# First attention block of a two-block decoder kernel: half of the modulation by dot products, and a new order of VectorE's, ScalarE's and TensorE's work in it

## What is computed

```python
mod = silu(c) @ ada_w[0] + ada_b[0]                  # 1024 -> 6 * 1024
sh1, sc1, g1, sh2, sc2, g2 = split(mod, 6)
h = rmsnorm(x, norm_g) * (1 + sc1) + sh1
proj = h @ w_in                                       # 1024 -> 384 + 256 + 32
c_q, c_kv = rmsnorm(proj[:, :384]), rmsnorm(proj[:, 384:640])
k_rope = apply_rope(proj[:, 640:])
q  = (c_q  @ w_uq ).reshape(256, 16, 64 + 32)         # rope on the last 32
kv = (c_kv @ w_ukv).reshape(256, 16, 64 + 64)         # k_nope, v
o = softmax(mask(q k^T * scale)) v                    # 16 heads, two blocks of 128 queries
x = x + g1 * (o @ w_out)
```

## Time and profile before

| | us |
|---|---|
| Median of three timed runs | 2814.59 |
| The profiled execution | 2818.61 |
| Its span | 2816.8 |
| PE busy / DVE busy / ACT busy | 2649.1 / 1961.2 / 1562.6 |

### The profile page before, as it was taken

The page is one execution under the profiler, slowest core; times in us unless marked ns, Lnnn a source line. Parts: engine busy times, 40 slices in busy tenths (PEclk is TensorE's granted clock), DMA queues, the critical chain, the costliest instruction groups (busy, mean ns, idle before and its releaser), DMA issues.

```text
span 2816.8 us, 39113 instructions
## 1 busy us (share of the span) xinstructions
PE 2649.1 (94%) x15496; PEld 2307.9 (82%) x15496; DVE 1961.2 (70%) x2819; ACT 1562.6 (55%) x2264; POOL 10.9 (0%) x24
## 2 busy tenths in 40 slices
PE   7788998888999999999996999999999999999998
PEld 3677998876788888888885998887898998887898
DVE  3768877766698898899897556655555556656555
ACT  2443445554687777777775445465444445465444
POOL 0000000000000000000000000000000000000000
PEclk9789998999899999999998999999999999999999
DMA  8537984514699999999996665534565665434563
GB/s 277 189 114 267 346 307 128 150 60 142 240 365 335 332 369 339 337 354 352 335 357 214 196 186 174 155 93 134 166 186 156 196 186 174 150 98 128 162 186 116
DMA packets 349600, 616.35 MB, mean 219 GB/s; under 512 B 20706, under 2 KB 174882, under 8 KB 349410
## 3 DMA queue, kind: packets, MB, share of 16 engines
q1 hardware_dynamic: 346402, 603.35, 64.4%
q0 software_dynamic: 1872, 5.99, 0.7%
q10 hardware_dynamic: 1136, 4.44, 0.4%
HBM read 612.66 MB, written 1.05 MB: 218 GB/s over the span
## 4 chain that ended last, share of the span: by engine, by line
PE 87%; DVE 7%; ACT 3%; issue 1%; DMA 1%; DVEq 0%; ACTq 0%
PE pb L286 25%; PE pb L287 25%; PE pb L288 25%; PE pb L292 9%; PE pb L408 2%; DVE parts L260 2%; ACT parts L245 1%; PE pb L2204 1%; PE pb L2660 1%; DMA X<-in_x 0%; DVE hTl L421 0%; DVE raw L625 0%; ACT pb L478 0%; DVE xn L509 0%; DVE xn L512 0%
## 5 line engine op out<-in xcount | busy, mean ns | idle before, releaser
L260 DVE TENSOR_TENSOR parts<-raw,parts 128x1024 fp32r<-128x1024 f32 (+2 forms) x1051 | 1264.7, 1216 | 593.1 <-ACT parts L245 559.2
L245 ACT ACTIVATE parts<-raw 128x1024 fp32r<-128x1024 f32 (+2 forms) x1051 | 1102.7, 1054 | 829.0 <-PE pb L288 706.4
L286 PE MATMUL pb<-parts,arenar 128*128 128x512 f32 (+2 forms) x1696 | 669.1, 395 | 14.7 <-DVE arenar L421 6.1
L287 PE MATMUL pb<-parts,arenar 128*128 128x512 f32 (+2 forms) x1696 | 650.7, 384 | 0.0
L288 PE MATMUL pb<-parts,arenar 128*128 128x512 f32 (+2 forms) x1696 | 649.8, 383 | 0.0
L286 PE MATMUL pb<-hTh,parts 128*128 128x256 f32 x1952 | 559.8, 287 | 7.4 <-DVE hTl L421 5.1
L287 PE MATMUL pb<-hTl,parts 128*128 128x256 f32 x1952 | 558.4, 286 | 0.0
L288 PE MATMUL pb<-hTh,parts 128*128 128x256 f32 x1952 | 558.3, 286 | 0.0
L286 PEld LDWEIGHTS pb<-hTh,parts 128*128 128x128 f32 x1952 | 381.4, 195 | 11.7 <-issue 7.2
L286 PEld LDWEIGHTS pb<-parts,arenar 128*128 128x128 f32 x1696 | 322.0, 190 | 80.7 <-issue 16.7
L287 PEld LDWEIGHTS pb<-hTl,parts 128*128 128x128 f32 x1952 | 381.3, 195 | 1.8
(11 more groups left out here) (286 smaller groups left out, 1972.4 us busy)
## 6 DMA issues: line engine op xcount, KB each, us to landing
raw<-in_moe_w_gate SPq DMA_DIRECT2D x176, 512.0 KB, 5.2
raw<-in_moe_w_up SPq DMA_DIRECT2D x176, 512.0 KB, 5.2
raw<-in_moe_w_down SPq DMA_DIRECT2D x176, 512.0 KB, 5.2
raw<-in_ffn_wg SPq DMA_DIRECT2D x88, 512.0 KB, 4.1
raw<-in_ffn_wu SPq DMA_DIRECT2D x88, 512.0 KB, 3.7
raw<-in_ffn_wd SPq DMA_DIRECT2D x88, 512.0 KB, 4.4
raw<-in_ada_wT SPq DMA_DIRECT2D x80, 512.0 KB, 5.2
raw<-in_w_in SPq DMA_DIRECT2D x72, 512.0 KB, 3.7
```

What stands on the lines that cost most here:

```text
L245: a.e.activation(self.part(t, 0), self.slot(t), ACT.Copy).then_inc(*a.up(self.c.hi, t.m))
L260: v.e.tensor_tensor(self.part(t, 1), self.slot(t), self.part(t, 0).bitcast(F32), ALU.subtract).then_inc(*v.up(self.c.lo, t.m))
L286: e.matmul(o, a[0], b[0], start=start, stop=False, skip_group_check=True)
L287: e.matmul(o, a[0], b[1], start=False, stop=False, skip_group_check=True)
```

## The change

It has five parts. (1) The shift's eight plain tiles are replaced by eight dot tiles of the same size. Four of them stand among the scale's eight tiles, four behind. VectorE makes their dots, TensorE only spreads the resulting columns over rows. (2) Dots get a walk of their own (`dots`); `low` can be told not to do those ahead of it, as long as an assertion holds that they are fewer than six tiles behind. (3) Before the loop, all latents are turned and cut as they come, the common key's rope is made before q's, its turned copy before the first kv product; the lows of m = 1 and 2 stand between the pieces of xn. (4) In the loop each slot begins with the head's maximum, then come sums, one low, dots, values; on ScalarE the exponentials stand ahead of the cut. `q_dve` and `kT_dve` follow slot h+2. (5) The 24 dot tiles have other places in the stream: one ahead of m = 4 to 10 and 12 to 14, two ahead of 15 to 21.

```diff
-    def low(self, v, times=1):
-        while times and self.n_low < len(self.tiles):
-            t = self.tiles[self.n_low]
-            self.n_low += 1
-            if t.kind == "dot":
-                v.wait_ge(*self.landed(t))
-                self.dot(v, t, self.slot(t))
...
+    def low(self, v, times=1, dots=True):
+        for t in self.cut[self.n_lo:self.n_lo + times]:
+            while dots and self.n_dot < len(self.dotted) and self.dotted[self.n_dot].n < t.n:
+                self.dots(v)
+            assert all(x.n > t.n - self.nraw for x in self.dotted[self.n_dot:]), t.label
...
+    def dots(self, v, times=1):
+        for t in self.dotted[self.n_dot:self.n_dot + times]:
+            self.n_dot += 1
+            v.wait_ge(*self.landed(t))
+            self.dot(v, t, self.slot(t))
...
-    FIRST = (2, 3, 0, 1)
+    FIRST = (2, 3)
...
+        shift = self.K.dot_tiles(0)
+        mixed = sum(([*scale[2 * i:2 * i + 2], shift[i]] for i in range(4)), [])
+        return mixed + self.K.dot_tiles(1)
...
+        for n in range(2):
+            b = K.c.bk[4 + n]
+            t.wait_ge(*K.c.dv.val(("col", n)))
+            t.wait_ge(*b.turn(("ada", n)))
+            for j in range(4):
+                m = mm1(t.e, b.t[:, j * P:(j + 1) * P], K.acols[:, 4 * n + j:4 * n + j + 1].to_broadcast([P, P]),
+                        K.C["ident"])
+            m.then_inc(*t.up(K.c.pe, ("ada", n)))
...
-        dots = {4: 1, 5: 1, 6: 1, 7: 1, 22: 1, 23: 1} | {m: 2 for m in range(13, 22)}
+        dots = {m: 1 for m in (4, 5, 6, 7, 8, 9, 10, 12, 13, 14)} | {m: 2 for m in range(15, 22)}
...
-    def slot_dve(self, v, h):
+    def slot_dve(self, v, h, lows=0, dots=0):
         if h < 16:
             self.att.max_dve(v, h)
         if 1 <= h <= 16:
             self.att.sums_dve(v, h - 1)
+        self.K.W.low(v, lows, False)
+        self.K.W.dots(v, dots)
...
# TensorE
         self.c_pe(t, 0)
+        self.c_pe(t, 4)
         self.q_pe(t, 0)
-        self.c_pe(t, 4)
-        self.kv_pe(t, 0)
         t.wait_ge(*c.dv.val("kr"))
         K.turn_pe(t, "krT", 6, [self.kr[:, tt, :] for tt in range(2)])
+        self.kv_pe(t, 0)
...
# ScalarE
         self.in_act(a, 0)
-        K.W.hi(a, 2)
         self.c_act(a, 0)
         self.in_act(a, 1)
+        self.c_act(a, 4)
         K.root_act(a, "c", slice(0, 4))
         K.W.hi(a, 2)
-        self.c_act(a, 4)
+        K.W.hi(a, 2)
...
+            self.slot_act(a, h)
             K.W.hi(a)
             self.kv_act(a, g)
-            self.slot_act(a, h)
-            K.W.hi(a)
             self.slot_act(a, h + 1)
             K.W.hi(a)
             self.slot_act(a, h + 2)
+            K.W.hi(a)
             self.slot_act(a, h + 3)
...
# VectorE
-        self.start.scale_dve(v)
+        K.W.dots(v, 2)
+        self.start.scale_dve(v, 0)
+        K.W.dots(v, 2)
+        self.start.scale_dve(v, 1)
+        K.W.dots(v, 4)
+        K.W.low(v)
         self.start.shift_dve(v)
-        K.W.low(v, NSPLIT - 2)
-        for key, b, tt, k0, hi, lo in self.x_pieces():
+        for i, (key, b, tt, k0, hi, lo) in enumerate(self.x_pieces()):
             K.parts_dve(v, key, b, hi, lo)
+            if i % 2:
+                K.W.low(v)
         K.W.low(v, 2)
         K.W.low(v, 4)
         self.in_dve(v, 0)
+        self.in_dve(v, 1)
+        self.c_dve(v, 0)
+        self.c_dve(v, 4)
+        self.roots_dve(v)
+        self.key_rope_dve(v)
         K.W.low(v, 2)
...
+        K.W.low(v, 2, False)
         (copy of krT)
+        self.q_dve(v, 0)
+        K.W.low(v, 1, False)
...
-            K.W.low(v)
-            self.slot_dve(v, h)
-            K.W.low(v)
-            self.slot_dve(v, h + 1)
-            K.W.low(v)
+            self.slot_dve(v, h, 1, 2)
+            self.slot_dve(v, h + 1, 1, 1 if g == 2 else 2)
+            self.slot_dve(v, h + 2, 1)
             self.q_dve(v, g)
             for j in range(2):
                 self.kT_dve(v, g, j)
-            self.slot_dve(v, h + 2)
-            self.slot_dve(v, h + 3)
+            self.slot_dve(v, h + 3, 0, 2)
```

More of the change, by code:

```diff
@@ L199, in __init__ @@
         self.cut = [t for t in tiles if t.kind == "w"]
+        self.dotted = [t for t in tiles if t.kind == "dot"]
         self.place = {t.label: n for n, t in enumerate(tiles)}
@@ L209, in rewind @@
     def rewind(self):
-        self.n_hi = self.n_lo = self.n_low = self.n_pe = self.n_sp = 0
+        self.n_hi = self.n_lo = self.n_dot = self.n_pe = self.n_sp = 0
     def shaped(self, x, t):
@@ L245, in hi @@
             a.e.activation(self.part(t, 0), self.slot(t), ACT.Copy).then_inc(*a.up(self.c.hi, t.m))
-    def low(self, v, times=1):
-        while times and self.n_low < len(self.tiles):
-            t = self.tiles[self.n_low]
-            self.n_low += 1
-            if t.kind == "dot":
-                v.wait_ge(*self.landed(t))
-                self.dot(v, t, self.slot(t))
-            if t.kind != "w":
-                continue
-            times -= 1
+    def low(self, v, times=1, dots=True):
[3 more added lines that the diff above has]
+            assert all(x.n > t.n - self.nraw for x in self.dotted[self.n_dot:]), t.label
             self.n_lo += 1
@@ L677, in tiles @@
         w = wview(self.K.A["ada_w"][0])
-        return [Tile(("ada", n, k0), w[:, k0:k0 + 2, n * 512:n * 512 + 512], (2, 512), "plain")
-                for n in self.FIRST for k0 in (0, 2, 4, 6)]
+        scale = [Tile(("ada", n, k0), w[:, k0:k0 + 2, n * 512:n * 512 + 512], (2, 512), "plain")
+                 for n in self.FIRST for k0 in (0, 2, 4, 6)]
+        shift = self.K.dot_tiles(0)
+        mixed = sum(([*scale[2 * i:2 * i + 2], shift[i]] for i in range(4)), [])
+        return mixed + self.K.dot_tiles(1)
     def sp(self, s):
@@ L735, in dve, with scale_dve @@
             K.stats_dve(v, "n0", tt)
-    def scale_dve(self, v):
+    def scale_dve(self, v, h):
         K, c, dv = self.K, self.K.c, self.K.c.dv
         v.wait_ge(*K.row_landed(0))
[L741 to L749, removed]
+        b, cs = c.bk[6 + h], slice(h * 512, (h + 1) * 512)
+        v.wait_ge(*c.pe.val(("ada", 2 + h)))
+        v.e.scalar_tensor_tensor(out=K.mod[:, 1, cs], in0=b.t[:, :], scalar=1.0, in1=K.row(0)[:, cs], op0=ALU.add,
+                                 op1=ALU.mult).then_inc(*v.up(b.out, ("ada", 2 + h)))
+        v.wait_ge(*v.tail)
+        for tt in range(2):
+            v.e.scalar_tensor_tensor(out=K.xn[:, tt, cs], in0=K.X[:, tt, cs], scalar=K.rst[:, tt:tt + 1],
+                                     in1=K.mod[:, 1, cs], op0=ALU.mult, op1=ALU.mult).then_inc(*v.up(dv))
     def shift_dve(self, v):
@@ L1170, in pe @@
         self.c_pe(t, 0)
+        self.c_pe(t, 4)
         self.q_pe(t, 0)
-        self.c_pe(t, 4)
-        self.kv_pe(t, 0)
-        b = c.bk[6]
         t.wait_ge(*c.dv.val("kr"))
         K.turn_pe(t, "krT", 6, [self.kr[:, tt, :] for tt in range(2)])
+        self.kv_pe(t, 0)
         for j in range(2):
@@ L1256, in dve @@
         self.in_dve(v, 0)
-        K.W.low(v, 2)
[L1258 to L1263, removed]
-        K.W.low(v)
-        self.key_rope_dve(v)
+        self.in_dve(v, 1)
[3 more added lines that the diff above has]
+        self.key_rope_dve(v)
+        K.W.low(v, 2)
+        K.W.low(v, 2, False)
         b = c.bk[6]
```

## The result

The changed kernel takes 2830.18 us (median of five runs, 2827.99 to 2831.3), the kernel before on the same chip 2816.22: **14.0 us slower, ratio 1.0047, interval 1.0034 to 1.0061**. Predicted were 2820, with a range from 2806 to 2829, so the time lies above the range. The profiled execution took 2828.48 us with a span of 2826.7. At the end of the first attention the two traces are 13.3 us apart (the row load behind it: 219.84 against 206.58) (the timed runs: 14.0). At the end of the two profiled executions it is 9.9 us; where behind the first attention the other 3.4 us go was not looked into, and no code is changed there.

The account below looks back on a forecast made before the run. It took TensorE to bound the start, then the latents, and in the loop waits ahead of exponentials. -12.4 + 5.1 + 12.65 + 0.3 = +5.7 us on 2818.61, a profile 4.0 above the median, gave 2820 us, range 2806 to 2829.

Parts of the forecast that it names:

- the term for the raw buffers: Loop: dots holding buffers make tiles m = 15, 16, 18, 19, 21, 22 late for ScalarE's cuts; 12.65 us.
- Start: Up to the first w_in matmul: two of TensorE's four products go, matmul at 47.6 instead of 56.18, 8.6 us earlier.
- Latents: Up to the loop: new order starts group 1's kv product at 88.0 instead of 100.82, 12.8 us earlier in all.
- The front: Everything ahead of the loop, start and latents: head 0's scores start at 91.7, 12.4 us earlier.
- Order of the loop: Head 0's to head 12's scores, without late tiles: 73.2 us against 68.1, 5.1 us longer.
- The nine waits: Loop, behind each maximum: VectorE waits for exponentials and cut, 1.2 to 1.75 us in each of three slots per group.
- Clock: TensorE: transposes count as work for the clock; longer pauses cost 0.3 us more after head 12.
- Tiles in time: Rival, loop: held buffers don't bite, no late tiles; -7 us, 2807.6 us; chance 0.12.
- Maximum first pays: Rival, loop: earlier exponentials shrink VectorE's waits, loop no longer than before; -12.1 us, 2802.5 us; chance 0.09.
- Front gives little: Rival, ahead of the loop: only half of the 12.4 us comes; +12 us, 2826 us; chance 0.17.
- From head 12 on: Behind the loop: same instructions, TensorE full, traces run alike; nothing counted.

Follow-up runs that it names:

- experiment 1: The changed kernel with only the dot tiles' places in the stream altered, so that they are used up in their order; 2812.64 us, ratio 0.9985.
- experiment 3: experiment 1 with ScalarE's cuts ahead of the exponentials again, VectorE still in the new order; 2795.74 us, ratio 0.9927.
- experiment 5: The changed kernel, its own dot tile places kept, with ScalarE's cuts back ahead of the exponentials; 2831.1 us, ratio 1.0057.

## Why the prediction was off

**Direction and mechanism were right, the size too small:** +5.7 us predicted, +13.6 at head 12, +14.0 timed. The step that failed is the term for the raw buffers, 12.65 us in the sum and 17.9 measured, because the landing of tiles asked for in a burst was taken too short.

**Start.** The scale's last product was to end near 34.5; VectorE went on at 34.18. Shift additions were to end at 45.3: 45.0. First w_in matmul 47.6: 46.58. The sixteen transposes of xn took 3.50 us (from 43.02 on) instead of 4.3.

**Latents.** 62.65 predicted, 63.31 measured; `q_dve` 81.65 against 83.08; kv product 88.0 against 89.65; head 0 at 91.7 against 92.94. The tile m = 12 was to cost 1 us; ScalarE had it at 78.42 and VectorE waited 1.48, and the rest is smaller sums. The front gave 11.2 instead of 12.4.

**Order of the loop.** Predicted 73.2 us of distance without late tiles; experiment 1, which is just that kernel, has 74.9. The nine waits were to be 1.2 to 1.75 us, they are 1.4 to 1.9. The net of 5.1 was right to 1.7 us, but its two halves are large: VectorE's new order takes 9.2 us off the old distance (experiment 3), the cut behind the exponential puts 16 back (experiments 1 and 3). That the net is close is therefore partly luck. I gave the sum and did not see that the gain in it could be had alone.

**Raw buffers: the step that failed.** "Sum 12.65 us" was 17.9. Term by term, predicted and measured: m = 15 3.35 and 4.21; 16 1.75 and 2.34; 18 1.55 and 1.81; 19 2.4 and 2.50; 21 2.9 and 4.27; 22 0.7 and 0.41. And "m = 17 and 20 have the length of a product and are in time": m = 17 is, m = 20 waits 2.37. The list of held buffers was right, the landing was not: I counted it from rows of one or two tiles, 3.6 and 4.5 us, but m = 15, 20 and 21 were each the third of three tiles asked for within some 1.5 us, and took 5.6, 6.5 and 6.1. m = 20 alone is 2.37 of the 5.25 us that were missing, m = 15 and 21 another 2.2: issued at 151.54, m = 20 was wanted at 155.70, so with a landing of 4.2 us it would have been in time as I had said. The bound that I had put down for this term, 18 us, is what came, but by luck: it was six tiles at 4.5 us each, and it was seven, three of them slower. 74.9 + 17.9 = 92.8 us, the measured distance (92.9). This sum comes out for this order of ScalarE's work; experiment 5 shows that the sum of the waits is no price in another. The errors: 1.2 (front) + 1.7 (order) + 5.25 (tiles) = 8.15, less 0.3 for the clock that is inside the distance, which is the 7.9 us between +5.7 and +13.6.

"DMA: Bandwidth & Descriptors" of the Trainium skill (Anatomy of one DMA) fits another issuing path than SP's; by it the estimate would be 3.2 us for 512 KB. No 512 KB load of this loop landed so soon: the shortest took 3.4 us, the median of the 14 dot tiles was 4.3 and of w_out's eight 4.6.

**Clock.** That turned transposes count as work was taken from a row, and the rows of 85.99 to 90.62 bear it out: after sixteen transposes only two matmuls (0.77 and 0.57) are long, the third has 0.40. The kernel before shows the other case: its first w_in matmul at 56.18 comes right behind 4.15 us of idle TensorE, with its transposes ahead of the pause, and eleven matmuls are long (the first, of 0.76 us, stands in the earlier trace rows):

```profile
56.74 0.63 PE L287 MATMUL pb<-parts,hTh 128*128 128x512 f32 x1
...
60.16 0.63 PE L286 MATMUL pb<-parts,hTh 128*128 128x512 f32 x1
60.58 0.49 PE L287 MATMUL pb<-parts,hTh 128*128 128x512 f32 x1
60.91 0.40 PE L288 MATMUL pb<-parts,hTl 128*128 128x512 f32 x1
```

By "TensorE: Matmul & The Clock Gate" of the Trainium skill (PE-mode transpose) the product behind the transposes would have been slow throughout; here it was not. The clock of the loop fell to 0.73, which I had not forecast, and which experiment 1 shows too (0.77 over its loop); what of it lies on the path is inside that kernel's 74.9 us and was not separated.

**Rivals.** Tiles in time: no, seven cuts waited. Maximum first pays: not in this kernel, but in experiment 3, with tiles in time and the cut ahead, the loop is 9.2 us shorter than the old one, where the rival had it only as long. Front gives little: no, 11.2 of 12.4.

**From head 12 on** the traces run alike: +13.6 at head 12, +13.3 at the end of the attention.

What stays open: whether the front, worth 16.6 us alone, is really worth only 11.3 with the new loop (24.5 - 13.2), since the intervals allow that both are the same. Head 0's start moved between 89.8 and 93.9 us over kernels with nearly the same front. Part of it is there at the start: the first dot that waits for its tile began between 27.51 and 29.26 us. So single profiles can't settle it.

## What to carry over

With a shared pool of load buffers filled in a fixed order, a consumer that is moved behind its place in the stream costs twice: it holds its buffer, and the loads behind it in the queue come late together. Move the tile in the stream when its use is moved; here that alone was 17.5 us, and 35 with the cut ahead of the exponential (2831.1 us in experiment 5, 2795.74 in experiment 3). And on the engine with the most work in a loop, put work that is ready between an operation and the answer that it waits for: a maximum, then dots, then the low that needs ScalarE. A cost measured in one arrangement says little for another: putting the cut back ahead was worth 17 us with tiles in time and nothing with tiles late.

## What the runs showed of the hardware

A 512 KB load took 3.6 us alone and 4.5 behind one other. As the third of three issued within some 1.5 us it took 5.6, 6.5 and 6.1 in the changed kernel, with the DMA engines busy 0.38 of the time over the loop, but 0.92, 0.64 and 0.63 while these three were on their way: the latency goes with the burst, not with the average. Why 6.5 and 6.1 us came with less traffic than 5.6, no run shows. The granted clock over the same 304 instructions of TensorE was 0.73 with long gaps and 0.89 with short ones (changed kernel, experiment 3), and they took 55.2 and 47.1 us of busy time; both lie between the levels of 1.2 and 2.4 GHz as means over stretches at either. A product behind 3.65 us of transposes had two long matmuls, one right behind 4.15 us of idle time (kernel before) had eleven.
